# Moved weight splits in three blocks, and the gathered tokens' expert values summed pick by pick on VectorE

## The chip, the cores and the metric

The kernel runs on one core of a Trainium2 chip. The metric is the device time of one execution in microseconds (us). The five engines are called by their names or by the short forms of the profile: TensorE (PE, its weight loads PEld), VectorE (DVE), ScalarE (ACT), GpSimd (POOL), and SyncE (SP), which here only issues DMAs.

## The reference

Two transformer blocks run one after the other on one sequence of 512 tokens with 1024 features, all in float32.

The first block: RMS norm; one projection to a gated convolution branch (31 taps) and to an attention branch with 8 heads of stick-breaking attention; output projection and residual; RMS norm, a gated feed-forward part of width 2816 with a 3-tap convolution, and residual.

The second block: RMS norm and one projection; differential attention and a native sparse attention with a compressed, a selected and a window branch; sigmoid gates, output projection, residual; cross attention to 256 memory tokens; and then the part that the change is about, a layer of experts:

```python
s = jnp.einsum('thcd,hcnd->thcn', q, sub_keys)       # 8 heads, 2 halves, 128 keys
top_s, top_i = lax.top_k(s, 16)
cand = top_s[:, :, 0, :, None] + top_s[:, :, 1, None, :]
best_s, best_j = lax.top_k(cand, 16)                 # 16 experts of 128*128 a head and token
g = softmax(best_s)
act = gelu(einsum('cd,chkd->chk', x, u_tab[expert])) # 128 picks a token
out = einsum('chk,chkd->cd', g * act, v_tab[expert])
```

So each token picks 8 x 16 = 128 of 16384 experts, and its result is the sum over these picks of a weight times a row of 1024 values. At the end stands an RMS norm.

## The kernel before

**Number format and splits.** Nearly all products are made of three float32r matmuls: each operand is split into a high part (a rounded copy, ScalarE) and a low part (operand minus high part, GpSimd for weights, VectorE for activations), and `al*bh + ah*bl + ah*bh` is summed in PSUM. Weights come in blocks of up to 128x2048 into two buffers `raw[g % 2]`. `split_hi(act, g)` (L240 on) waits for the load and for TensorE to be done with block g - 2, and writes `w_hi`; `split_lo` (L253) writes `w_lo`, in the order of the blocks. TensorE (`linear_pe`, `products`, L261 to L263) waits for the low part of each block. As every engine executes its program in order, the place where a `split_hi` stands in ScalarE's program decides when the next block is ready.

**Places of these splits that matter here.** `block1_act`: the input projection `in_fm` (8 blocks of two 128-row tiles); for its first four pairs of tiles (j) ScalarE waits until VectorE has drained a pair, makes a sigmoid and then splits block j + 2; VectorE meanwhile works through a 31-tap convolution (`conv_dve`, L482), five taps behind each drained tile. `in_v`, the projection of the values, has eight tiles; `spread_pair` (L658) is a small matmul of TensorE behind tiles 2 to 5 that needs the reciprocal `rstd16` (L821) of VectorE, and `normalised` scales queries and keys by it. `first_scores` stands behind tile 6. `up0` is the first half of the feed-forward: behind each pair of tiles ScalarE makes a silu, a high part and then a split. `splits_gained` splits the next block and writes the high parts and squares of the residual for the next norm. `block2_act` holds the sigmoid of 24 gates (L1106), two exponentials (L1109, L1111) and `hidden(1)`, a gelu (L1096) that TensorE waits for (L1278). In the cross attention loop VectorE scales the exponentials of one unit (L1658), ScalarE exponentiates and copies the transposed ones; one weight split stands behind the loop's second step.

**The experts.** 384 of the 512 tokens (NT) are computed densely, the first 128 (GT) by gathers.

Dense, first half (the u stage): for each of 128 chunks c of 128 experts SP loads `u_raw` (512 KB), ScalarE and GpSimd split it, TensorE multiplies it with the 384 tokens (24 matmuls of 384 columns), ScalarE takes the gelu, SP stores it to a scratch (192 KB). Chunks 0 to PRE - 1 (PRE = 36) run while VectorE works out the picks (`places`, `mark_places`, `keys`, for four groups of 128 tokens); the next 72 chunks run between matmuls that build the table of gate weights (L2178, two batches of 8 tokens for three chunks), which needs `rows_b` of ScalarE (L2033) and `rows_a` of VectorE; the table goes to a scratch in pieces of 1 MB (`store_g`). The last 20 chunks stand alone. At FETCH_AT, chunk 120, SP begins to load what the second half needs.

Gathered tokens, first half: GpSimd issues 128 indirect DMAs (`gather_u`, L1918), one for each pick, that bring one row of 1024 values per token into a ring of seven buffers; `gathers_by(c)` says how many are issued by chunk c, and each stands in GpSimd's program behind `split_u_lo(c)`. Gather 4 waits until the keys of all four groups are there. VectorE makes the dot product of each row with the token (L2383, the token in PSUM). A gather waits for the dot seven before it.

Second half (the value stage): for each chunk c SP loads `h_raw` (192 KB, the stored gelu) and `v_raw` (512 KB), and for eight chunks at once `g_in` (1.5 MB of gate weights). VectorE multiplies h_raw by its gates (`weighted`, L2424) and makes its low part (`weighted_low`, L2428), ScalarE the high parts (L1943, L1952), GpSimd `v_lo` (L1947). All four have four buffers. TensorE adds 3 x 3 x 2 matmuls of 512 columns per chunk into three pairs of PSUM banks (`outputs`, L2208). ScalarE splits chunk c as soon as TensorE is done with chunk c - 4.

Gathered tokens, second half: for each of 32 steps i GpSimd issues four indirect DMAs (L1930) of rows of the value table, indexed by `idx_v`, the transpose of the picks, so that in each buffer all 128 partitions hold the picks of one token. TensorE multiplies them with 32 columns of a block-diagonal weight matrix `w_diag` (`gathered`, 16 matmuls, L2219) behind every fourth chunk, in plain float32, into the banks `y_acc`. `w_diag` comes from a memset of 128x4096 and four copies out of a transpose of the weights. At the very end VectorE adds the residual, and the last norm is made.

**What sets the order.** All of it is written out by hand, engine by engine, with counting semaphores; there is no planner. `peer_credits` gives the ring buffers their first credits.

The change touches, besides these places, `gather_v`, `ug_loaded` and the semaphores of the rows, `block3_pool`, `turn` (which transposed `idx_f` too), and `residual`, which takes the gathered tokens' sum out of PSUM.

## Time and profile before

| | us |
|---|---|
| three runs: median (lowest, highest) | 2587.88 (2580.64, 2592.19) |
| the profiled execution, its own time | 2588.76 |
| its span, first to last instruction | 2587.0 |
| TensorE busy | 2494.9 |
| VectorE busy | 1623.5 |
| GpSimd busy | 1363.2 |
| ScalarE busy | 1004.6 |
| data moved by DMA | 477.61 MB, mean 185 GB/s |

Busy time is the time in which an engine executes something; it contains stalls inside an instruction. The timeline and the chain of waits are in microseconds from the start of the span. "Idle before" names the engine and line whose completion ended an engine's idle time. The chain of waits is followed back from the last instruction, at each step to what released it. "PEclk" is the granted clock of TensorE as a share of its full 2.4 GHz; its other level is 1.2 GHz. The DMA share is the mean busy share of 16 DMA engines.

### The profile page before, as it was taken

Reading aid. Unit: us, or ns where it says so; the run is one execution under the profiler, and the core shown is the slowest. Engines: PE = TensorE matmul, PEld = TensorE weight load, DVE = VectorE, ACT = ScalarE, POOL = GpSimd, SP = SyncE. Lnnn points to the kernel's source line nnn. Section 1 sums busy time; section 2 is a strip of 40 time slices with the busy share of each in tenths; the row PEclk is TensorE's granted clock in tenths of the full one; section 3 lists DMA queues with packets and bytes.
Section 4 is the critical chain, followed back from the end, with each engine's and each line's share of the span. In section 5 each row is a group of like instructions: output and inputs, shape, how many; then the busy total and the mean of one; then the engine's idle time right before and its main releaser. Section 6 shows DMA issues by size and latency. Waiting matters only on the chain.

```text
span 2587.0 us, 34189 instructions
## 1 busy us (share of the span) xinstructions
PE 2494.9 (96%) x13105; PEld 2080.4 (80%) x13105; DVE 1623.5 (63%) x2822; ACT 1004.6 (39%) x1768; POOL 1363.2 (53%) x698
## 2 busy tenths in 40 slices
PE   6999899999999999998999989999999999999998
PEld 5765788888887666886899889999998677777776
DVE  4967654153224766645999967777746666666665
ACT  3236322123213655334444345555533233333333
POOL 3422355454432112442436666666677777777774
PEclk9989999999999999999999999999999999999999
DMA  3200222222421011322225579999999988888884
GB/s 133 81 33 17 74 91 91 102 97 83 180 98 50 17 36 47 123 105 82 82 89 174 186 243 319 332 331 331 332 357 341 345 329 310 313 303 326 313 311 179
DMA packets 151781, 477.61 MB, mean 185 GB/s; under 512 B 14688, under 2 KB 47840, under 8 KB 140640
## 3 DMA queue, kind: packets, MB, share of 16 engines
q1 hardware_dynamic: 114784, 341.64, 37.3%
q0 software_dynamic: 36864, 134.23, 14.4%
q8 instruction: 78, 1.28, 0.2%
q14 instruction: 55, 0.45, 0.1%
HBM read 423.39 MB, written 52.43 MB: 184 GB/s over the span
## 4 chain that ended last, share of the span: by engine, by line
PE 75%; DVE 16%; ACT 3%; DMA 2%; POOL 2%; issue 2%; SPq 0%; ACTq 0%; DVEq 0%
PE bank_pair L2208 19%; PE bank_pair L261 13%; PE bank_pair L263 13%; PE bank_pair L262 13%; PE bank_pair L2178 3%; DVE cacc L482 2%; PE bank_pair L2219 2%; PE bank_pair L1298 1%; PE bank_pair L684 1%; PE bank_pair L1333 1%; DMA u_raw<-expert_u 1%; POOL w_lo L253 1%; DVE one_hot L2325 1%; PE bank_pair L1349 1%; PE bank_pair L272 1%
## 5 line engine op out<-in xcount | busy, mean ns | idle before, releaser
L253 POOL TENSOR_TENSOR w_lo<-w_raw,w_hi 128x2048 fp32r<-128x2048 f32 (+2 forms) x95 | 420.4, 4426 | 597.6 <-ACT w_hi L248 597.4
L1905 POOL TENSOR_TENSOR u_lo<-u_raw,u_hi 128x1024 fp32r<-128x1024 f32 x128 | 313.3, 2448 | 192.5 <-ACT u_hi L1901 192.2
L1947 POOL TENSOR_TENSOR v_lo<-v_raw,v_hi 128x1024 fp32r<-128x1024 f32 x128 | 309.7, 2424 | 112.3 <-ACT v_hi L1943 111.7
L2428 DVE TENSOR_TENSOR h_lo<-h_raw,h_hi 128x384 fp32r<-128x384 f32 x128 | 251.5, 1965 | 184.7 <-ACT h_hi L1952 184.5
L261 PE MATMUL bank_pair<-uh,u_lo 128*128 128x384 f32 x1024 | 352.1, 344 | 13.9 <-POOL u_lo L1905 13.5
L263 PE MATMUL bank_pair<-uh,u_hi 128*128 128x384 f32 x1024 | 343.5, 335 | 0.0
L262 PE MATMUL bank_pair<-ul,u_hi 128*128 128x384 f32 x1024 | 343.5, 335 | 0.0
L1943 ACT ACTIVATE v_hi<-v_raw 128x1024 fp32r<-128x1024 f32 x128 | 135.6, 1060 | 384.5 <-PE bank_pair L2208 353.1
L248 ACT ACTIVATE w_hi<-w_raw 128x2048 fp32r<-128x2048 f32 (+2 forms) x96 | 174.6, 1819 | 274.3 <-PE bank_pair L263 258.9
L261 PE MATMUL bank_pair<-xh,w_lo 128*128 128x512 f32 x624 | 247.6, 397 | 18.8 <-POOL w_lo L253 16.7
L1901 ACT ACTIVATE u_hi<-u_raw 128x1024 fp32r<-128x1024 f32 x128 | 135.6, 1060 | 334.7 <-PE bank_pair L263 302.5
L263 PE MATMUL bank_pair<-xh,w_hi 128*128 128x512 f32 x624 | 245.0, 393 | 0.0
L262 PE MATMUL bank_pair<-xl,w_hi 128*128 128x512 f32 x624 | 244.8, 392 | 0.0
L2208 PE MATMUL bank_pair<-v_lo,h_hi 128*128 128x512 f32 x768 | 240.8, 395 | 1.3 <-DVE h_lo L2428 1.3
L2208 PE MATMUL bank_pair<-v_hi,h_lo 128*128 128x512 f32 x768 | 237.3, 390 | 0.0
L2208 PE MATMUL bank_pair<-v_hi,h_hi 128*128 128x512 f32 x768 | 236.9, 390 | 0.0
L261 PEld LDWEIGHTS bank_pair<-uh,u_lo 128*128 128x128 f32 x1024 | 193.6, 189 | 18.7 <-POOL u_lo L1905 16.4
L262 PEld LDWEIGHTS bank_pair<-ul,u_hi 128*128 128x128 f32 x1024 | 193.6, 189 | 0.0
L263 PEld LDWEIGHTS bank_pair<-uh,u_hi 128*128 128x128 f32 x1024 | 193.0, 188 | 0.0
L2208 PEld LDWEIGHTS bank_pair<-v_lo,h_hi 128*128 128x128 f32 x768 | 141.7, 188 | 55.4 <-issue 25.1
L2383 DVE CUSTOM_DVE_ANT_0 ug<-bank_pair,ug 128x1024 f32<-128x1024 f32 x128 | 151.7, 1218 | 46.2 <-DMA ug<-expert_u_rows,idx_u 46.2
L2208 PEld LDWEIGHTS bank_pair<-v_hi,h_lo 128*128 128x128 f32 x768 | 144.2, 188 | 30.9
(445 smaller groups left out, 5170.3 us busy)
## 6 DMA issues: line engine op xcount, KB each, us to landing
w_raw<-w_small SPq DMA_DIRECT2D x80, 1024.0 KB, 4.8
u_raw<-expert_u SPq DMA_DIRECT2D x128, 512.0 KB
v_raw<-expert_v SPq DMA_DIRECT2D x128, 512.0 KB, 6.5
h_scratch<-h_act SPq DMA_DIRECT2D x128, 192.0 KB
g_scratch<-stage SPq DMA_DIRECT2D x24, 1024.0 KB, 6.2
g_in<-g_scratch SPq DMA_DIRECT2D x16, 1536.0 KB, 13.4
h_raw<-h_scratch SPq DMA_DIRECT2D x128, 192.0 KB, 5.8
w_raw<-w_small SPq DMA_DIRECT2D x8, 768.0 KB, 4.2
```

The source lines that it names most:

```text
L248: act.activation(wh[g % 2][:, :n], raw[g % 2][:, :n], ACT.Copy).then_inc(sem("hi_done"), 1)
L253: pool.tensor_tensor(wl[g % 2][:, :n], raw[g % 2][:, :n], wh[g % 2][:, :n].bitcast(F32), ALU.subtract).then_inc(sem("lo_done"), 1)
L261: pe.matmul(out, al, bh, start=(k == 0), stop=False)
L262: pe.matmul(out, ah, bl, start=False, stop=False)
L263: last = pe.matmul(out, ah, bh, start=False, stop=(k == len(pairs) - 1))
L1901: act.activation(u_hi[c % 2][:, :, :], u_raw[c % 4][:, :, :], ACT.Copy).then_inc(sem("u_hi"), 1)
L1905: pool.tensor_tensor(u_lo[c % 2][:, :, :], u_raw[c % 4][:, :, :], u_hi[c % 2][:, :, :].bitcast(F32), ALU.subtract)\
L1943: act.activation(v_hi[c % 4][:, :], v_raw[c % 4][:, :], ACT.Copy).then_inc(sem("v_hi"), 1)
L1947: pool.tensor_tensor(v_lo[c % 4][:, :], v_raw[c % 4][:, :], v_hi[c % 4][:, :].bitcast(F32), ALU.subtract)\
L2208: last = pe.matmul(acc[tt][:, cols], h[s][:, tokens], v[s][:, cols], start=start and n == 0, stop=stop and n == 2)
L2383: dve.tensor_tensor_reduce(out=rows[:, :], in0=x_tok[:, :], in1=rows[:, :], scale=1.0, scalar=0.0, op0=ALU.mult, op1=ALU.add, accum_out=do ...
L2428: dve.tensor_tensor(h_lo[c % 4][:, :], h_raw[c % 4][:, :], h_hi[c % 4][:, :].bitcast(F32), ALU.subtract)\
```

## The change

In words, in the order of the program:

1. `splits_gained`: where a block has four tiles (`cross_o`), the split of the block after next stands before the fourth tile of the block, not before its first.
2. `in_fm`: block 2 is split ahead of `norm_std`; each later split stands one step earlier.
3. `in_v`: the spreads stand behind tiles 3 to 6, the first scores behind tile 6 want only six of eight scaled tiles; the last spread pair stands behind them and writes to two banks of `lin_bank`.
4. `up0`: block 2 is split right behind `norm_std`, each later one a step earlier.
5. Block 2: the two exponentials stand before the gate sigmoids, and VectorE waits for the gates where it uses them.
6. Cross attention: the second split of `cross_v` stands behind the loop.
7. Experts: PRE is 40 (20 single chunks at the end become 16), FETCH_AT stays at chunk 120, gathers of the first half go on from chunk 37, with 7 per 5 chunks instead of 4 per 3.
8. The rows of the value table are gathered with the index of the first half, one pick of all 128 tokens per DMA, into a ring of eight buffers: eight in the first four chunks, then as `rows_asked_by` says. VectorE multiplies each by the pick's weight (one scalar per partition) and adds it in PSUM, `picks_by(c)` of them by chunk c, from chunk 8 to 127. `gathered`, `w_diag`, `idx_v` and the transposes for them are gone.

```diff
@@ splits_gained
-                if b < t["nb"] - 1:
+                if b < t["nb"] - 1 and t["tiles"] < 4:
                     split_hi(act, t["block"] + b + 2)
                 for k in range(b * t["tiles"], (b + 1) * t["tiles"]):
+                    if b < t["nb"] - 1 and k % t["tiles"] == 3:
+                        split_hi(act, t["block"] + b + 2)
@@
-        SPREAD_TILES = (2, 3, 4, 5)
+        SPREAD_TILES = (3, 4, 5, 6)
 
         def spread_bank(n):
-            return att_bank[3 - n % 2]
+            return att_bank[3 - n % 2] if n < 6 else lin_bank[n - 6]
@@ block1_act
+            base = LAYER["in_fm"]["block"]
+            split_hi(act, base + 2)
             act.wait_ge(sem("consts"), N_CONST)
             norm_std(act, "n1", norm_stat1, S)
-            base = LAYER["in_fm"]["block"]
             for j in range(CT):
...
-                split_hi(act, base + j + 2)
+                split_hi(act, base + j + 3)
             for j in range(4):
                 if j < 3:
-                    split_hi(act, base + 4 + j + 2)
+                    split_hi(act, base + 4 + j + 3)
...
-            split_hi(act, base + 4 + 3 + 2)
@@
             norm_std(act, "n2", norm_stat2, S)
+            split_hi(act, LAYER["up0"]["block"] + 2)
...
-                    split_hi(act, up["block"] + b + 2)
+                    if half:
+                        split_hi(act, up["block"] + b + 2)
+                    elif b < FHALF[0] - 1:
+                        split_hi(act, up["block"] + b + 3)
@@ block1_pe
             def first_scores(pe):
-                pe.wait_ge(sem("qk_ready"), len(PAIR_ORDER))
+                pe.wait_ge(sem("qk_ready"), 6)
                 scores(0)
+                pe.wait_ge(sem("bank_free"), 4 + LAYER["in_v"]["tile"] + 6)
+                spread_pair(3)(pe)
...
-            pe.wait_ge(sem("bank_free"), 4 + LAYER["in_v"]["tile"] + 7)
+            wait(pe, ("bank_free", 4 + LAYER["in_v"]["tile"] + 7), ("qk_ready", len(PAIR_ORDER)))
             scores(1)
@@ block2_act
+            act.wait_ge(sem("lam_sum"), 1)
+            act.activation(lam_exp[:, :], att_bank[3][:, 0:2], ACT.Exp).then_inc(sem("lam_exp"), 1)
+            act.wait_ge(sem("cmp_sub"), 1)
+            act.activation(cmp_s[:, :, :, :], cmp_s[:, :, :, :], ACT.Exp).then_inc(sem("cmp_exp"), 1)
             norm_wait(act, "n3", "diag", 1, 1)
...
-            act.wait_ge(sem("lam_sum"), 1)
-            act.activation(lam_exp[:, :], att_bank[3][:, 0:2], ACT.Exp).then_inc(sem("lam_exp"), 1)
-            act.wait_ge(sem("cmp_sub"), 1)
-            act.activation(cmp_s[:, :, :, :], cmp_s[:, :, :, :], ACT.Exp).then_inc(sem("cmp_exp"), 1)
             hidden(1)
@@
-                if s == 1:
-                    splits("cross_v", 1)
...
+            splits("cross_v", 1)
             splits_gained(act, "cross_o", "n5", pq_h, "norm_ffn")
@@
             chain.link(dve.reciprocal(rec2, stat2))
+            dve.wait_ge(sem("bank_free"), 4 + MIXED)
             chain.link(dve.tensor_tensor(cmp_rec[:, :, :], cmp_rec[:, :, :], gates24[:, :, 0::3], ALU.mult))
@@
-        PRE = 36
+        PRE = 40
-        FETCH_AT = PRE + MID + 12
+        FETCH_AT = PRE + MID + 8
         def gathers_by(c):
 
-            if c < 33:
+            if c < 37:
                 return max(0, min(UG_EARLY, c - 18))
-            return min(P, UG_EARLY + (c - 31) * 4 // 3)
+            return min(P, UG_EARLY + (c - 35) * 7 // 5)
@@
+        def picks_by(c):
+
+            return max(0, min(P, (c - 7) * 16 // 15))
+
+        def rows_asked_by(c):
+
+            return min(len(vg), 2 * (c + 1)) if c < 10 else min(P, picks_by(c - 2) + len(vg))
+
+        def gather_v(pool, j):
+
+            b = j % len(vg)
+            if j == 0:
+                pool.wait_ge(sem("u_used"), 2 + NK)
+            if j >= len(vg):
+                pool.wait_ge(sem("vg_used"), j - len(vg) + 1)
+            pool.indirect_dma_start(vg[b][:, :], None, v_rows, bass.IndirectOffsetOnAxis(idx_u[:, j:j + 1], 0))\
+                .then_inc(sem(vg_loaded(j)[0]), 16)
@@ block3_pool
-            for k in range(QUADS):
-                for n in range(4):
-                    split_v_lo(pool, 4 * k + n)
-                for i in {0: (0,), 1: (1,), 2: (2, 3)}.get(k, (k + 1,)):
-                    if i < QUADS:
-                        gather_v(pool, i)
+            for c in range(NK):
+                split_v_lo(pool, c)
+                for j in range(rows_asked_by(c - 1), rows_asked_by(c)):
+                    gather_v(pool, j)
@@ block3_pe
-                if i == 0:
-                    pe.transpose(lin_bank[0][:, 3 * P:4 * P], idx_f[:, :], ident[:, :])
...
-            def gathered(i):
-
-                pe.wait_ge(sem("w_step"), 3)
-                pe.wait_ge(sem(f"vg_loaded{i % 2}"), 16 * VQ * (i // 2 + 1))
-                for half in range(2):
-                    for q in range(VQ):
-                        w = w_diag[:, (i * VQ + q) * 32:(i * VQ + q + 1) * 32]
-                        last = pe.matmul(y_acc[half][32 * q:32 * q + 32, :], w, vg[i % 2 * VQ + q][:, half * S:(half + 1) * S],
-                                         start=(i == 0), stop=(i == NK // VQ - 1))
-                last.then_inc(sem("vg_used"), 1)
@@ block3_dve
+            def picked(j):
+                b = j % len(vg)
+                wait(dve, vg_loaded(j))
+                w = w_tok[:, j:j + 1]
+                if j == 0:
+                    dve.wait_ge(sem("w_step"), 1)
+                    ins = dve.tensor_scalar(y_tok[:, :], vg[b][:, :], w, None, ALU.mult)
+                else:
+                    dve.wait_ge(sem("vg_used"), j)
+                    ins = dve.scalar_tensor_tensor(out=y_tok[:, :], in0=vg[b][:, :], scalar=w, in1=y_tok[:, :],
+                                                   op0=ALU.mult, op1=ALU.add)
+                ins.then_inc(sem("vg_used"), 1)
+
             weighted(0)
             for c in range(NK):
                 weighted(c + 1)
                 weighted_low(c)
-                if c == 3:
-                    dve.wait_ge(sem("u_lo"), 4 + NK)
-                    link(dve.memset(w_diag[:, :], 0.0))
...
+                for j in range(picks_by(c - 1), picks_by(c)):
+                    picked(j)
```

## Rows read from the trace of the kernel before

**Rows 1.** The page's first part: busy us (share of the span) xinstructions.

```profile
PE 2494.9 (96%) x13105; PEld 2080.4 (80%) x13105; DVE 1623.5 (63%) x2822; ACT 1004.6 (39%) x1768; POOL 1363.2 (53%) x698
```

**Rows 2.** Chain that ended last, value stage: start us, us, engine, output, line.

```profile
2042.61 1.85 PE bank_pair L2219 x16
2044.47 16.59 PE bank_pair L2208 x72
2579.74 1.24 DVE out_sb L2452
```

**Rows 3.** Instructions of L2208: ns min/median/max, first and last start us.

```profile
L2208 PE MATMUL bank_pair<-v_lo,h_hi x768: 388/389/505, 1984.3 to 2578.4; 128*128 128x512 f32 x192
```

**Rows 4.** Timeline of PE: start us, us, what, [idle before it <-who ended it].

```profile
47.72 0.79 PE L261 MATMUL bank_pair<-xh,w_lo 128*128 128x512 f32 x1 [9.23 <-POOL w_lo L253]
...
136.20 3.78 PE L658 MATMUL bank_pair<-rstd,head_spread 16*128 16x512 f32 x4 [3.77 <-DVE rstd L821]
...
320.65 0.79 PE L261 MATMUL bank_pair<-xh,w_lo 128*128 128x512 f32 x1 [6.92 <-POOL w_lo L253]
...
818.66 1.03 PE L1278 MATMUL bank_pair<-cmp_w,cmp_hid 128*16 128x64 f32 x8 [3.09 <-ACT cmp_hid L1096]
...
1181.15 0.69 PE L1422 MATMUL bank_pair<-ident,ca_e 128*128 128x128 f32 x2 [2.85 <-DVE ca_e L1658]
...
1220.74 0.79 PE L261 MATMUL bank_pair<-ca_h,w_lo 128*128 128x512 f32 x1 [2.43 <-DVE resid L759]
...
1489.23 0.69 PE L261 MATMUL bank_pair<-uh,u_lo 128*128 128x384 f32 x1 [4.22 <-POOL u_lo L1905]
...
1503.95 2.07 PE L2178 MATMUL bank_pair<-rows_b,rows_a 128*128 128x128 f32 x8 [4.10 <-ACT rows_b L2033]
...
2022.44 3.62 PE L2219 MATMUL bank_pair<-vg,w_diag 128*32 128x512 f32 x16 [2.41 <-DMA vg<-expert_v,idx_v]
```

**Rows 5.** Chain that ended last, around the first of these idle times.

```profile
39.25 0.69 DVE cpad L786
48.51 0.43 PE bank_pair L262
```

**Rows 6.** The same chain, before the second of them.

```profile
132.89 3.27 DVE rstd L821
```

**Rows 7.** Timeline of DVE, cross attention.

```profile
1177.06 4.04 DVE L1658 TENSOR_SCALAR ca_e<-ca_e,ca_stat 128x256 f32<-128x256 f32 x1
```

**Rows 8.** Three kinds of VectorE instruction: duration ns min/median/max.

```profile
L2383 DVE CUSTOM_DVE_ANT_0 ug<-bank_pair,ug x128: 1210/1219/1227, 1490.5 to 1972.6; 128x1024 f32<-128x1024 f32 x128
...
L482 DVE SCALAR_TENSOR_TENSOR cacc<-cpad,params_sb,cacc x120: 729/741/5098, 63.6 to 225.6; 128x512 f32<-128x512 f32 x120
...
L2428 DVE TENSOR_TENSOR h_lo<-h_raw,h_hi x128: 544/2450/7104, 1976.5 to 2560.5; 128x384 fp32r<-128x384 f32 x128
```

**Rows 9.** Groups, 2100 to 2500 us: count, busy us, mean ns, idle before.

```profile
L2428 DVE TENSOR_TENSOR h_lo<-h_raw,h_hi 128x384 fp32r<-128x384 f32 x87 | 172.4, 1982 | 134.0 <-ACT h_hi L1952 134.0
L2424 DVE TENSOR_TENSOR h_raw<-h_raw,g_in 128x384 f32<-128x384 f32 x87 | 94.9, 1091 | 6.6 <-DMA h_raw<-h_scratch 6.6
...
L1947 POOL TENSOR_TENSOR v_lo<-v_raw,v_hi 128x1024 fp32r<-128x1024 f32 x87 | 209.8, 2414 | 81.2 <-ACT v_hi L1943 80.8
L1930 POOL DMA_INDIRECT vg<-expert_v,idx_v x88 | 86.6, 984 | 24.0 <-issue 23.2
```

**Rows 10.** DMA of 2100 to 2560 us: total; issues, KB each, landing us.

```profile
DMA packets 51899, 142.06 MB, mean 309 GB/s; under 512 B 4912, under 2 KB 17328, under 8 KB 51873
v_raw<-expert_v SPq DMA_DIRECT2D x97, 512.0 KB, 7.3
g_in<-g_scratch SPq DMA_DIRECT2D x12, 1536.0 KB, 13.4
h_raw<-h_scratch SPq DMA_DIRECT2D x97, 192.0 KB, 4.9
```

**Rows 11.** A stretch: PE, PEld, DVE, ACT, POOL busy, PEclk, DMA share, GB/s.

```profile
1900.00:1950.00 50.00, 47.76 (x270) 46.26 (x269) 19.00 (x32) 16.26 (x22) 40.33 (x26) 1.00 1.03 402
```

More of the change, by code:

```diff
@@ L1754, in ug_loaded @@
             b, full = j % UG, 16 * (j // UG + 1)
-            return f"ug_loaded{b}", full
-        VQ = 4
+            return f"row_loaded{b}", full
         vg = [at(f"vg{i}", [P, D], o) for i, o in enumerate(
@@ L1919, in gather_u, with vg_loaded @@
                 .then_inc(sem(ug_loaded(j)[0]), 16)
[L1921 to L1931 removed]
+        def vg_loaded(j):
+            b = j % len(vg)
+            before = len(range(b, P, UG)) if b < UG else 0
+            return f"row_loaded{b}", 16 * (before + j // len(vg) + 1)
+        def picks_by(c):
+            return max(0, min(P, (c - 7) * 16 // 15))
+        def rows_asked_by(c):
+            return min(len(vg), 2 * (c + 1)) if c < 10 else min(P, picks_by(c - 2) + len(vg))
+        assert picks_by(NK - 1) == P and rows_asked_by(NK - 1) == P
+        def gather_v(pool, j):
+            b = j % len(vg)
+            if j == 0:
+                pool.wait_ge(sem("u_used"), 2 + NK)
+            if j >= len(vg):
+                pool.wait_ge(sem("vg_used"), j - len(vg) + 1)
+            pool.indirect_dma_start(vg[b][:, :], None, v_rows, bass.IndirectOffsetOnAxis(idx_u[:, j:j + 1], 0))\
+                .then_inc(sem(vg_loaded(j)[0]), 16)
         def gelu(act, c):
@@ L2230, in block3_pe @@
                     last.then_inc(sem("out_done"), 1)
-                    if c == 4:
-                        pe.wait_ge(sem("w_step"), 1)
-                        pe.transpose(y_acc[0][:, 0:P], w_tok[:, :], ident[:, :]).then_inc(sem("w_step"), 1)
-                if q == 1:
-                    gathered(0)
-                if q >= 1:
-                    gathered(q)
-            gathered(QUADS - 1)
             for c in range(NK - 4, NK):
```

27 lines of the change are left out of this document (5 added, 22 removed).

## The prediction

> **What bounds the kernel now.** I read the page first: TensorE is busy 96% of the span [rows 1], so a change pays where it takes TensorE work or TensorE idle time away. Second the chain of waits over the last stage, in which every chunk of experts' values is multiplied in. There it is TensorE alone, in a rhythm of 16.59 us for the 72 `outputs` matmuls of four chunks and 1.85 us for the 16 matmuls of one `gathered` step [rows 2]; nobody waits in between. Third the timeline of PE with its idle times, which shows where the splits come late [rows 4]. The reader should see in it that nearly all idle time lies in single gaps with one named releaser each.
>
> **The value stage.** Its first matmul starts at 1984.3 [rows 3] and VectorE takes the last result at 2579.7 [rows 2]: 595.4 us. Of this 32 x 16.59 = 530.9 are `outputs`, 32 x 1.85 = 59.2 are `gathered`, and the second `gathered` step also waited 2.4 us for its rows and then ran 3.62 instead of 1.85 us [rows 4], 4.2 us together; the 1.1 us left are two short waits. The change deletes `gathered`, with the wait, the transpose and the 4096-wide diagonal matrix. 59.2 + 4.2 = 63.4 us leave TensorE.
> What is added: 128 picks on VectorE, each 128x1024, one input in SBUF, the other and the output in PSUM. No row shows this form. Nearest is the dot of L2383, 128x1024 with one input in PSUM: 1219 ns, and never above 1227 though GpSimd was subtracting beside it [rows 8]. The other end is the multiply-add of L482 with both inputs in SBUF, 741 ns for half the elements and up to 5098 ns when it meets GpSimd [rows 8]. I take the dot, 1.25 us with the wait for the pick before. 16/15 pick per chunk is 1.33 us; TensorE will need 16.59/4 = 4.15 us per chunk.
> VectorE: it is now busy 1.98 + 1.09 = 3.07 us per chunk with h_lo and h_raw [rows 9]. With the picks that would be 4.40, over 4.15. But most of the 3.07 is stall: alone each takes about 0.55 us (the minimum of L2428 is 544 ns [rows 8]; the two have one form but for the output's type), and they are long where they meet GpSimd's v_lo (2.41 us [rows 9]). GpSimd's 2.41 and 1.1 of VectorE exclude each other, 3.5 of 4.15 us; the pick can run beside v_lo, and VectorE's work without stall is 1.1 + 1.33 = 2.4. A steady order exists: v_lo beside a pick, then h_raw and h_lo, then the next pick. h_lo also has three chunks (12 us) before TensorE needs it. So I price VectorE at nothing; if the stalls stay as they are, the stage is paced at 4.40, 128 x 0.25 = 32 us more.
> GpSimd: v_lo 2.41 and 16/15 gathers of 0.98 + 0.27 of issue [rows 9], 3.75 of 4.15 us. It fits, with little left. A gather waits for the pick eight before it, and v_lo is queued behind it; the program asks only for rows whose buffer was picked two chunks earlier, so this wait should be over.
> DMA: per chunk v_raw 524 KB, h_raw 197 KB, an eighth of g_in 197 KB [rows 10] and 16/15 row gather of 524 KB, 559 KB: 1.477 MB in 4.15 us is 356 GB/s. Now it is 309 GB/s [rows 10]. A stretch of 50 us ran at 402 GB/s [rows 11], so I price it at nothing; v_raw lands in 7.3 us and has about 13 us before it is late.
> The Trainium skill (DMA: Bandwidth & Descriptors, Specifications) puts the HBM limit of one core at about 358 GB/s. By it the stage would sit at its limit, with no reserve. The 402 GB/s of [rows 11], where most of the traffic is also reads, disagree with it, with one core at work.
> New cost at the start: two gathers now stand behind each of v_lo 0 to 3, where before all four v_lo came first. Two gathers are 2.5 us, v_lo with them 4.9 against 4.15: about 0.7 us late three times, 2 us. Bounds 0 and 5. Term: 63.4 - 2 = 61 us saved.
>
> **The moved splits.** Each removes a gap of TensorE and what the gap costs after it. After the first one the chain has the matmuls at 0.43 us [rows 5], the step of the lower of the engine's two clocks; at the full clock they take 16.59/72 = 0.23 [rows 2]. Some twelve ran so: 12 x 0.2 = 2.4 us.
> - in_fm: `split_hi(base + 2)` no longer stands behind the first sigmoid. The gap of 9.23 [rows 4] was ACT's split and then GpSimd's. The next limit is VectorE's drain of tile 0, done at 39.25 + 0.69 [rows 5]; the gap begins at 47.72 - 9.23 = 38.5, so 1.5 us stay. 7.7 + 2.4 = 10. VectorE's convolution, which paces the rest of in_fm, begins only after tile 5, so it moves along. Bounds 5 and 12.
> - in_v: the spreads stand one tile later, tile 3 fills the gap of 3.77 [rows 4]. VectorE's reciprocal ends at 132.89 + 3.27 = 136.2 [rows 6] and is not moved by this, and one more weight split may meet the convolution ahead of it. Gap and slow clock together are 7; I take 4, bounds 0 and 7. What is late next: the last pair's spread, with tile 7 still to cover it.
> - up0: `split_hi(block + 2)` right behind norm_std, no longer behind the whole chain of convolution, silu and product of the first pair of tiles; ScalarE and GpSimd then have the time of two tiles for it, which is more than they need. 6.92 [rows 4] + 2.4 = 9.3. ScalarE's next pieces wait for VectorE anyway. Bounds 6 and 10.
> - exps of the compressed branch before the gate sigmoids: the subtraction they need is done while TensorE still works on mix_tm, so they move beside it. hidden(1) no longer queues behind two exps and a table load; the gap of 3.09 [rows 4] shrinks by an estimated 2, and VectorE's chain of softmax steps behind it, which starts earlier, by a little more. Term 2.7, bounds 0 and 4.
> - cross attention: GpSimd's w_lo no longer meets the row scaling, which took 4.04 us for 256 columns [rows 7] (512 columns with two inputs take 741 ns [rows 8]) and made the gap of 2.85 [rows 4]; with the slow clock behind it 4.3. The split now comes behind the loop, with the first four tiles of cross_o to cover it. cross_o's split stands behind three gained tiles, not before the first: the gap of 2.43 [rows 4] and some slow matmuls go, 3.7. Together 8, bounds 3 and 10.
>
> **PRE 36 to 40, gathers from chunk 37.** At chunk 34 TensorE waited 4.22 us because GpSimd's u_lo stood behind gather 4, which waits for the last keys [rows 4]; that gather now stands four chunks later. 4.2 + 2.2 of slow clock, a little less than above as its tiles are shorter, = 6.4. The 4.10 us before the first table [rows 4] stay: ACT makes the rows only behind the gelu of the last chunk before it, wherever PRE is. The rate 7/5 instead of 4/3 adds 2% of traffic in the middle stage; store_g comes four chunks nearer to the fetch at 120, and SP waits for it there with the next u_raw queued behind it. Bounds of the whole: gain 8, loss 3.
>
> **Sum.** 61 + 10 + 4 + 9.3 + 2.7 + 8 + 6.4 = 101 us. The profiled execution took 2588.8 us (its span 2587.0 and 1.8 around it), 0.9 above the median of the runs shown, 2587.9. 2588.8 - 101 = 2487.8; against the median 2487. With every small piece a chance to fall short and none to give more, I say 2489.
>
> **Rivals.**
> A. The value stage gets a new pace. VectorE keeps its stalls (4.40 us per chunk) or the DMA settles at 340 GB/s (1.477 MB in 4.34 us): 25 to 32 us are given back, 2514 to 2521. For it: VectorE's sum above 4.15, GpSimd at 3.75, the DMA need 15% above today's. Against: buffers of four chunks and eight rows, the stretch at 402 GB/s. A half of it gives 2503.
> B. The early gaps close but a chain behind them takes the time back: VectorE's convolution in in_fm, the top-k chain that paces chunks 25 to 33, DMA at the end of the u stage. Then of the 40 us outside the value stage perhaps 15 remain: 2514.
> C. Slower: the pick behaves as L482, not as the dot, taking GpSimd's port for its SBUF operands. Then it waits out v_lo each time: 16/15 x (1.25 + 2.41) = 3.9, with 3.07 already there 7.0 us per chunk, 128 x 7.0 = 896 instead of 531, 2853. If all only exclude each other, 2.41 + 1.1 + 1.33 = 4.84 per chunk, 88 us more, 2577. It decides for slower from (531 + 101)/128 = 4.94 us per chunk on. Against it: the pick has one operand in SBUF, like the dot.
> The Trainium skill (SBUF: State Buffer, Who interferes with whom) says that a VectorE instruction with two SBUF inputs contends with a GpSimd instruction that reads SBUF, and one with at most one does not. The 1227 ns of the dot agree; no row has a pick with its output in PSUM.
> D. The change doesn't do what it says: rows arrive late because of the eight buffers, VectorE stands in a pick and h_lo behind it. A row is asked for 5.5 chunks (23 us) before its pick; with landings of some 10 us it holds. It would look like A.
>
> **How the numbers follow.** Forecast 0.64, with its own range 2478 to 2502 (the bounds of the small terms, not all at one end). A with D 0.18, B 0.12, C 0.03 (of it 0.02 slower), something unseen 0.03. The range 2474 to 2524 takes in A and B. What a measurement can tell from no change is 0.5%, 13 us: faster 0.96, same 0.02, slower 0.02.
>
> **What would show it.** In the profile after: no L2219, the chain in the value stage as L2208 without a break, 16.6 us per four chunks, the stage 533 us long; picks of 1.2 us; VectorE near full but mostly in stalls; DMA near 350 GB/s; TensorE idle below 3 us at the places of [rows 4], but 4 us before the first table. The prediction is wrong if L2208 shows waits for h_lo or v_lo in the value stage, or picks well above 1.3 us, or if gaps of the early stages return under other names.

## The result

The kernel before took 2585.18 us (median of 4 runs), the changed kernel 2504.29 us (2503.76 to 2509.48, 4 runs), ratio 0.968 [0.9644, 0.9715]. The forecast was 2489 with a range of 2474 to 2524. So the change makes the kernel faster, by 81 us in the medians and by 84.3 us between the two profiled executions (2588.8 and 2504.5), where the sum said 101. The table below accounts for the missing 17.

### The profile page after: what moved, and what is told of

The parts are those of the page before. It is cut to its first block, busy times and chain, and to the rows that moved or that the text cites. A ratio compares the mean times of both kernels' runs of the same rounds, so it can differ in the third digit from the quotient of the medians.

```text
span 2502.7 us, 33378 instructions
## 1 busy us (share of the span) xinstructions
PE 2422.7 (97%) x12591; PEld 2066.0 (83%) x12591; DVE 1729.9 (69%) x2944; ACT 1006.3 (40%) x1768; POOL 1376.9 (55%) x698
## 4 chain that ended last, share of the span: by engine, by line
PE 57%; DVE 22%; issue 9%; DMA 8%; POOL 2%; ACT 2%; SPq 0%; DVEq 0%; ACTq 0%
PE bank_pair L261 14%; PE bank_pair L262 13%; PE bank_pair L263 13%; DVE bank_pair L2435 4%; PE bank_pair L2193 3%; DMA h_raw<-h_scratch 3%; DVE h_lo L2423 2%; DVE cacc L484 2%; DMA u_raw<-expert_u 2%; DMA g_in<-g_scratch 1%; PE bank_pair L1305 1%; DVE one_hot L2321 1%; PE bank_pair L1340 1%; PE bank_pair L690 1%; PE bank_pair L272 1%
## 5 line engine op out<-in xcount | busy, mean ns | idle before, releaser
L2419 DVE TENSOR_TENSOR h_raw<-h_raw,g_in 128x384 f32<-128x384 f32 x128 | 263.3, 2057 | 39.8 <-DMA h_raw<-h_scratch 39.7
L2223 PEld LDWEIGHTS bank_pair<-v_hi,h_hi 128*128 128x128 f32 x768 | 144.7, 188 | 30.2
```

The costliest lines, as they stand in the source:

```text
L2223: last = pe.matmul(acc[tt][:, cols], h[s][:, tokens], v[s][:, cols], start=start and n == 0, stop=stop and n == 2)
L2419: dve.tensor_tensor(h, h, g_in[c // OCT % 2][:, :, c % OCT, :], ALU.mult).then_inc(sem("h_f"), 1)
```

## The profile after

First the page's line of busy times, which answers to [rows 1]:

```profile
PE 2422.7 (97%) x12591; PEld 2066.0 (83%) x12591; DVE 1729.9 (69%) x2944; ACT 1006.3 (40%) x1768; POOL 1376.9 (55%) x698
```

Then the value stage, by stretch (columns: window, its length, busy us and instructions of PE, PEld, DVE, ACT, POOL, the granted clock, the DMA engines' busy share, GB/s):

```profile
2000.00:2450.00 450.00, 450.00 (x1987) 372.59 (x1986) 433.66 (x340) 163.25 (x220) 392.68 (x228) 1.00 0.98 362
```

TensorE doesn't pause once in 450 us, beside a VectorE that is busy for 96% and DMA engines for 98%. The two costliest lines of VectorE in it, asked by line over the whole trace (duration in ns: shortest/median/longest, then the start of the first and the last, in us):

```profile
L2435 DVE SCALAR_TENSOR_TENSOR bank_pair<-vg,w_tok,bank_pair x127: 1274/1277/1290, 2001.0 to 2478.3; 128x1024 f32<-128x1024 f32 x127
L2419 DVE TENSOR_TENSOR h_raw<-h_raw,g_in x128: 543/2238/3343, 1950.0 to 2470.8; 128x384 f32<-128x384 f32 x128
```

The pick is 1.28 us, never more than 1.29 (forecast 1.25; the slower rival C is out). h_raw bears the stall: its median is four times its shortest, and in the timeline it stands beside GpSimd's v_lo (h_raw from 2242.05 for 3.33 us, v_lo from 2242.55 for 2.41).

The timeline of PE's waits, which answers to [rows 4] (start, duration, instruction; in brackets the idle time before it and who ended it):

```profile
40.00 0.50 PE L261 MATMUL bank_pair<-xh,w_lo 128*128 128x512 f32 x1 [1.51 <-DVE cpad L794]
117.45 3.60 PE L654 MATMUL bank_pair<-qk_sq,head_sum 128*16 128x512 f32 x4 [3.75 <-ACT qk_sq L527]
306.14 0.79 PE L261 MATMUL bank_pair<-xh,w_lo 128*128 128x512 f32 x1 [6.92 <-POOL w_lo L253]
802.23 0.62 PE L1285 MATMUL bank_pair<-cmp_w,cmp_hid 128*16 128x64 f32 x8 [1.09 <-ACT cmp_hid L1104]
806.23 0.49 PE L1305 MATMUL bank_pair<-ka,qa 64*128 64x128 f32 x4 [2.36 <-DVE cmp_pt L1538]
809.25 1.22 PE L1305 MATMUL bank_pair<-ka,qa 64*128 64x256 f32 x3 [1.63 <-DVE att_stat L1551]
1464.50 0.87 PE L2170 MATMUL bank_pair<-ident,chosen 128*128 128x128 f32 x3 [5.21 <-DVE chosen L2338]
1496.52 2.07 PE L2193 MATMUL bank_pair<-rows_b,rows_a 128*128 128x128 f32 x8 [4.13 <-ACT rows_b L2050]
1947.89 0.44 PE L261 MATMUL bank_pair<-uh,u_lo 128*128 128x384 f32 x1 [2.05 <-POOL u_lo L1910]
1968.01 0.73 PE L2223 MATMUL bank_pair<-v_lo,h_hi 128*128 128x512 f32 x2 [0.81 <-POOL v_lo L1966]
2477.19 0.70 PE L2223 MATMUL bank_pair<-v_lo,h_hi 128*128 128x512 f32 x2 [4.13 <-DVE h_lo L2423]
```

Gone against [rows 4]: 9.23, 3.77, both waits of the cross attention, 4.22 at chunk 34 and the wait for gathered rows. Stayed: 6.92 at up0, and 4.1 before the first table (as forecast). New: 3.75, 5.21, 4.13, and four short waits for v_lo at the start of the value stage, the first of which is shown.

Where the 84.3 us come from. The savings are differences of one event's start in the two traces, given in brackets or behind "to", before first. The first table comes at 1503.95 and 1496.52; in the changed kernel four more chunks of the u stage, 16.6 us, stand ahead of it and four fewer behind, so these are added and taken off:

| stretch | forecast | saved |
|---|---|---|
| start to the matmul that waits for mix_h (249.31, 234.79): in_fm, in_v | 14 | 14.5 |
| up0 | 9.3 | 0 |
| exps of the compressed branch, to 837.57 and 822.65 | 2.7 | 0.4 |
| cross attention, to 1403.86 and 1379.81 | 8 | 9.1 |
| PRE and gathers, to the first table, less the four chunks | 6.4 | 0 |
| end of the u stage, to the first value matmul (1984.3, 1962.9) | 0 | -2.7 |
| value stage (595.4, 532.5) | 61 | 63 |

## The experiments

**One half of the change at a time.** e1_value_only is the kernel before with the gathered values summed on VectorE, its splits, PRE and u gathers untouched; e2_splits_only the reverse, the changed kernel with the value stage, PRE and the u gathers taken back. The cores of the two, e1 against the kernel before and e2 against the changed one:

```diff
-                if q >= 1:
-                    gathered(q)
-            gathered(QUADS - 1)
...
+                for j in range(picks_by(c - 1), picks_by(c)):
+                    picked(j)
```

```diff
-                for j in range(picks_by(c - 1), picks_by(c)):
-                    picked(j)
...
+            gathered(QUADS - 1)
...
-        PRE = 40
+        PRE = 36
```

> Only the pick-by-pick sum of the gathered tokens, on the old order of everything else and PRE 36. My theory (the gathered matmuls were pure TensorE time, VectorE, GpSimd and DMA cover the picks): 59 + 4 us leave, 2 come back at the start of the value stage and some 5 at its end, where VectorE is late: about 58 to 62 us less than before, 2523 to 2529. Rival (part of the gain needs the other edits, by more DMA reserve in the value stage with the earlier gathers): under 50 us, above 2535.

> Only the moved splits of the two blocks, the spreads, the exponentials and the cross attention, on the old last block (PRE 36, matmul sum). Theory from the trace of the changed kernel: 24 us less than before, 14.5 of them by the attention of the first block, 0 in up0, 0.4 at the exponentials, 9 in the cross attention; 2562 to 2566. My prediction on record had 34 for these; the rival that it stands for (the loss lies in the last block, not here) gives 2554.

Measured beside a median of 2590.81 before: e1 2528.54, ratio 0.976 [0.9739, 0.9776], 62 us; e2 2566.70, 0.991 [0.9892, 0.9927], 24 us. The halves add up to 86, and the changed kernel's 2504.29 is 86 us under the same median, so they don't work against each other. The missing 17 us lie outside the value stage: the moved splits bring 24 where the sum had 34, and the 6.4 for PRE and the gathers, which e2 has not, did not come (e3).

**PRE and the gathers put back.**

```diff
-        PRE = 40
+        PRE = 36
...
-        FETCH_AT = PRE + MID + 8
+        FETCH_AT = PRE + MID + 12
...
-            if c < 37:
+            if c < 33:
...
-            return min(P, UG_EARLY + (c - 35) * 7 // 5)
+            return min(P, UG_EARLY + (c - 31) * 4 // 3)
```

> The changed kernel with PRE 36, 4 gathers per 3 chunks from chunk 33, as before. Theory (moving the gathers frees GpSimd, whose subtractions then meet VectorE's key reduction, so what TensorE gains behind gather 4 it loses at the turn of the keys): no change, within 4 us of the changed kernel, and in the trace the wait for chosen back at about 1 us and the one behind gather 4 back at about 4 us. Rival (my prediction): the edit is worth 6.4 us, so this kernel is 6 slower.

2505.70, 0.968 [0.9659, 0.9697]: the same as the changed kernel. In its trace the old pair of waits is back:

```profile
1456.88 0.52 PE L2170 MATMUL bank_pair<-ident,chosen 128*128 128x128 f32 x3 [1.12 <-DVE chosen L2338]
1461.63 0.69 PE L261 MATMUL bank_pair<-uh,u_lo 128*128 128x384 f32 x1 [4.23 <-POOL u_lo L1910]
```

1.12 + 4.23 in this order, 5.21 in the changed one: one wait changed its name. The edit can be read at its place too: from the matmul that waits for mix_h to the first value matmul it takes 1727.6 us here and 1728.1 in the changed kernel.

**Why it changed its name.** e7_hold_pool keeps PRE at 40 and only lets GpSimd ask for a row early, so that it stands still at chunk 33 again.

```diff
-                return max(0, min(UG_EARLY, c - 18))
+                return max(0, min(UG_EARLY, c - 18)) + (c >= 33)
```

> The changed kernel, PRE stays at 40, but from chunk 33 on each gather of u rows is asked for one chunk earlier, so that GpSimd stands waiting for the keys at chunk 33 as before the change and makes no u_lo meanwhile. Theory (the two engines' shared access to SBUF makes the key selection slow): the three reductions of the last key selection take 2.4 instead of 6.5 us, TensorE's wait for chosen is near 1.1 instead of 5.21 us, and a wait of about 4.2 us for u_lo stands behind it: total 2502 to 2507, no gain. Rival (it is PRE at 40, which puts other matmuls ahead of the last scores, that makes chosen late): the reductions stay at 6.5 and the wait at 5.2, with the u_lo wait added, 2508 to 2512.

First the changed kernel: VectorE's three folding additions of the last key selection (L2321), and GpSimd beside them:

```profile
1456.96 6.51 DVE L2321 TENSOR_TENSOR one_hot<-one_hot 128x2048 bf16<-128x2048 bf16 x3
1456.31 2.86 POOL L1910 TENSOR_TENSOR u_lo<-u_raw,u_hi 128x1024 fp32r<-128x1024 f32 x1 [1.53 <-ACT u_hi L1906]
1460.53 2.67 POOL L1910 TENSOR_TENSOR u_lo<-u_raw,u_hi 128x1024 fp32r<-128x1024 f32 x1 [1.35 <-ACT u_hi L1906]
```

Then e7_hold_pool, VectorE, GpSimd and TensorE:

```profile
1461.93 2.41 DVE L2321 TENSOR_TENSOR one_hot<-one_hot 128x2048 bf16<-128x2048 bf16 x3
1465.51 0.95 POOL L1923 DMA_INDIRECT ug<-expert_u_rows,idx_u  x1 [5.76 <-DVE chosen L2338]
1465.38 0.52 PE L2170 MATMUL bank_pair<-ident,chosen 128*128 128x128 f32 x3 [1.13 <-DVE chosen L2338]
1468.89 0.50 PE L261 MATMUL bank_pair<-uh,u_lo 128*128 128x384 f32 x1 [2.98 <-POOL u_lo L1910]
```

The additions fall from 6.51 to 2.41 us with nothing changed but GpSimd's standing still, and the wait of 5.21 to 1.13. The rival (PRE's order makes the keys late) is out. From the wait at 1441.69 (the last for u_lo before these) to the first table it takes 58.5 us, in the changed kernel 59.8 (from 1436.74). The run's 2508.24 (0.970 [0.9677, 0.9723]) can't tell 1.3 us from nothing.

**The third transpose of keys later.**

```diff
-        TURN_AT = (25, 29, 33)
+        TURN_AT = (25, 29, 36)
```

> The changed kernel with the third transpose of the chosen keys behind chunk 36 instead of chunk 33, some 12 us later on TensorE. Theory: TensorE's wait of 5.21 us for the last key selection goes, and the slow matmuls behind it (about 2 us): 5 to 7 us less, 2497 to 2499. Rival: the first gathers and the table's rows hang on that transpose, and what is won comes back as a longer wait before the first table (4.13 us now) or at GpSimd's u_lo behind the gathers: 2502 to 2506.

The wait of 5.21 is gone, one of 2.81 for u_lo at 1487.49 is in its place, 4.10 before the first table stays. The same stretch takes 56.9 us, 2.9 less. The time, 2508.10 (0.970 [0.9676, 0.9722]), missed the expected 2497 to 2499: elsewhere this run was slower. Its profile has TensorE at mix_h 5.25 us later than the changed kernel's, ahead of every edited line, and 6.5 instead of 4.13 us of waiting at the very end.

**up0.** ScalarE's split of the second block now starts at 287.46, early enough, as forecast. GpSimd's doesn't. In the changed kernel:

```profile
287.46 1.91 ACT L248 ACTIVATE w_hi<-w_raw 128x2048 fp32r<-128x2048 f32 x1
299.55 1.57 POOL L636 TENSOR_TENSOR fl<-f_out,fh 128x512 fp32r<-128x512 f32 x1 [15.46 <-ACT fh L599]
301.07 4.94 POOL L253 TENSOR_TENSOR w_lo<-w_raw,w_hi 128x2048 fp32r<-128x2048 f32 x1
```

GpSimd stood idle for 15.46 us, the last 10.2 of them with the finished w_hi (289.37) at hand, because `split_lo` is written behind its wait for the first product. e4_pool_up0 moves that:

```diff
             j = 0
+            split_lo(pool, LAYER["up0"]["block"] + 2)
...
-                    split_lo(pool, up["block"] + b + 2)
+                    if half:
+                        split_lo(pool, up["block"] + b + 2)
+                    elif b < FHALF[0] - 1:
+                        split_lo(pool, up["block"] + b + 3)
```

> The changed kernel with GpSimd's low parts of the up0 weights moved a step earlier too, as ScalarE's high parts are. Theory (the 6.92 us wait of TensorE stayed because GpSimd's split_lo stood behind the wait for ff_hi): the gap goes to under 0.5 us and 9 us leave in all with the slow clock behind it. Rival (TensorE then waits there for the next thing, bank or norm): gap stays over 3 us, gain under 5.

```profile
290.96 4.59 POOL L253 TENSOR_TENSOR w_lo<-w_raw,w_hi 128x2048 fp32r<-128x2048 f32 x1 [5.36 <-ACT w_hi L248]
301.06 1.60 POOL L637 TENSOR_TENSOR fl<-f_out,fh 128x512 fp32r<-128x512 f32 x1 [5.51 <-ACT fh L599]
```

TensorE waits there no more. From mix_h to cmp_hid it needs 558.2 us (236.32 to 794.57), the changed kernel 567.4: 9.2 saved, where the prediction had 9.3. In the time 5 arrived (2499.05, 0.965 [0.963, 0.9668]); in its trace a first load that landed 1.2 us later and a wait of 6.67 instead of 4.13 at the very end took most of the rest.

**The exps put back** (the four lines of the two `Exp` behind the sigmoids again, and VectorE's added wait out).

> The changed kernel with the two exps of the compressed branch behind the gate sigmoids again, as before the change. Theory (moving them only exchanged one wait for another, 0.4 us net): TensorE waits 3.1 us for cmp_hid and 1.5 for cmp_pt instead of 1.1, 2.4 and 1.6; the stretch between the waits for mix_h and for the first att_pt transpose (from 234.8 to 974.4 in the changed kernel) is 0 to 1 us longer. Rival (the move is worth the 2.7 us forecast): 2 to 3.5 us longer there. The total can't tell it, it varies by more.

```profile
803.44 0.62 PE L1285 MATMUL bank_pair<-cmp_w,cmp_hid 128*16 128x64 f32 x8 [3.09 <-ACT cmp_hid L1104]
```

With 1.54 for cmp_pt, and none for att_stat. The stretch from mix_h to the first att_pt takes 741.3 us, in the changed kernel 739.6, in the kernel before 740.0. So the edit is worth 1.7 by this run and 0.4 by before and after; it stands between the two expectations, and one execution doesn't settle it. Both are under the 2.7 forecast.

**The wait at the end.** In the kernel before, the last two `gathered` steps stood right ahead of the last four chunks:

```profile
2558.86 3.64 PE L2219 MATMUL bank_pair<-vg,w_diag 128*32 128x512 f32 x32
2563.10 0.70 PE L2208 MATMUL bank_pair<-v_lo,h_hi 128*128 128x512 f32 x2 [0.59 <-DVE h_lo L2428]
```

TensorE asks for h_lo and v_lo of all four chunks before the first matmul, and v_hi of chunk 127 can't begin before chunk 123 is done. The 3.64 us covered most of that: with the 0.59 behind them they make 4.23. Without them 4.13 are bare, and behind them the 72 matmuls take 18.22 us instead of 16.32. In six other runs of this value stage (e1, e3, e4, e5, e7, e9) the wait was 6.5 to 6.7. e12_tail_order asks chunk by chunk:

```diff
-            for c in range(NK - 4, NK):
-                outputs_ready(c)
             for tt in range(NT // P):
                 for c in range(NK - 4, NK):
+                    if tt == 0:
+                        outputs_ready(c)
...
```

> The changed kernel, but in the last four chunks TensorE waits for each chunk's h_lo and v_lo just ahead of that chunk's first matmuls, not for all four before the first. Theory (the wait near the end is one of program order: v_hi of chunk 127 may only start when chunk 123 is done, so v_lo and h_lo of it come 3.5 to 4 us later at the earliest, and the two gathered steps that stood there before the change, 3.64 us, covered it): the 18 matmuls of chunks 124 to 126 for the first tokens, 18 x 0.23 = 4.15 us, take the place of that cover; the wait of 4.13 to 6.5 us shrinks to 0 to 2.4, and the slow matmuls behind it (about 1.5 us) go or shrink: 4 to 6 us less than the changed kernel on this chip, 0.9655 to 0.967 of the kernel before. Rival (VectorE is behind by its own work or by late loads, whatever the order): the wait comes back in full at the last chunk, under 1 us less.

```profile
2475.15 0.70 PE L2223 MATMUL bank_pair<-v_lo,h_hi 128*128 128x512 f32 x2 [1.50 <-DVE h_lo L2423]
2479.43 0.70 PE L2223 MATMUL bank_pair<-v_lo,h_hi 128*128 128x512 f32 x2 [2.67 <-DVE h_lo L2423]
```

From the second value chunk's first matmul to the end of the last it takes 528.1 us; the six with a wait of 6.5 took 529.4 to 532.0, the changed kernel's own profile 527.4. The run's time is that of the changed kernel, 2504.29 (0.968 [0.9667, 0.9701]), so the expected 4 to 6 us did not come. With the floor of the order gone 4.17 us of waiting are left, for h_lo of chunks 125 and 126: VectorE is late by itself, as the rival of this run has it. Two of ScalarE's lines of the same trace suggest from where:

```profile
2449.58 1.06 ACT L1962 ACTIVATE v_hi<-v_raw 128x1024 fp32r<-128x1024 f32 x1 [7.25 <-DMA v_raw<-expert_v]
2474.57 0.52 ACT L1971 ACTIVATE h_hi<-h_raw 128x384 fp32r<-128x384 f32 x1 [3.88 <-DVE h_raw L2419]
```

Some 45 us before the end ScalarE stood idle for 7.25 us until a v_raw landed; in e5 the chain that ended last goes through a v_raw of 14.40 us (2434.86) at the same place. My reading, not shown, is that the chunks behind it then come close together, GpSimd's v_lo beside VectorE's h_raw, and that VectorE has not regained its lead when the last four chunks are due.

**DMA or VectorE?** Two kernels relieve one of them. e10_half_rows gathers only 64 of the 128 rows from pick 8 on, e11_half_picks adds only 512 of the 1024 columns.

```diff
+            r = P if j < len(vg) else P // 2
-            pool.indirect_dma_start(vg[b][:, :], None, v_rows, bass.IndirectOffsetOnAxis(idx_u[:, j:j + 1], 0))\
+            pool.indirect_dma_start(vg[b][0:r, :], None, v_rows, bass.IndirectOffsetOnAxis(idx_u[0:r, j:j + 1], 0))\
```

> The changed kernel, but from pick 8 on only the rows of tokens 0 to 63 are gathered (half of each gather's bytes; tokens 64 to 127 get old rows, so the sum of these is left out). Per chunk 280 KB less: 1.197 MB in 4.15 us, 289 GB/s instead of 356. Theory (the DMA queues are what lets VectorE fall behind): in the changed kernel VectorE waited 39.7 us for h_raw and TensorE 4.13 us for h_lo at 2477, with slow clock behind it; with less to move, the waits for h_raw nearly vanish (under 5 us), the wait for h_lo at the last four chunks is gone, and the time is 5 to 8 us below the changed kernel, 2497 to 2500. Rival (VectorE's own work with its port waits is the pace): waits for h_raw vanish but h_raw's own duration grows in their place, the wait for h_lo stays at 4 to 6.5 us, time 2503 to 2506.

> The changed kernel, but from pick 1 on only 512 of the 1024 columns are multiplied in (the other half of the sum is left out); all rows are still gathered whole. A pick falls from 1.28 to about 0.7 us, 0.6 us per chunk less on VectorE. Theory (DMA): VectorE waits longer for h_raw in place of it, some 40 + 70 us, and the wait for h_lo near the end is halved at most, 2500 to 2505. Rival (VectorE's own work): the wait for h_lo is gone, 5 to 8 us less, 2497 to 2500, while the waits for h_raw grow less than the picks shrink.

e10: 2509.51 (0.970 [0.9674, 0.9725]), a wait of 9.03 at the end. Both theories missed, and the window says why this was no relief:

```profile
2000.00:2450.00 450.00, 450.00 (x1987) 372.63 (x1986) 406.48 (x337) 166.40 (x219) 385.17 (x228) 1.00 1.01 291
```

The rate fell from 362 to 291 GB/s, the engines' busy share rose from 0.98 to 1.01, and ScalarE's waits for v_raw (2000 to 2500) from 41.7 to 175.2 us. A gather of half the rows does not cost half (the last section has its price). e11: 2509.20 (0.970 [0.9666, 0.9723]); the pick takes 744 ns, h_raw's median falls to 546 ns, VectorE waits 20.7 instead of 15.4 us for the loads, the end's wait is 4.13, the stretch to the end 528.1 us. Both expectations missed here too. And the relief was smaller than planned: h_lo took over the stall, its mean rose from 0.65 to 1.76 us, and VectorE's busy time from 2000 to 2450 fell by 22 us (433.7 to 411.6), 0.2 us per chunk and not 0.6. In the middle of the stage VectorE's work isn't the bound, as TensorE is busy for all 450 us in both. Whether it is what makes 6.5 of 4.13 at the end is not shown: e11 has 4.13, but so has the changed kernel's own profile, with whole picks. What costs the lead may be the DMA, as ScalarE's late v_raw suggests; no run relieved that, and it stays open.

**The sum in SBUF**, rival C made real.

```diff
-        x_tok = y_tok = bank_pair[2]
+        x_tok = bank_pair[2]
+        y_tok = at("y_tok", [P, D], RAW)
...
                     dve.wait_ge(sem("w_step"), 1)
+                    dve.wait_ge(sem("u_lo"), 4 + NK)
```

> The changed kernel, but the sum of the gathered values is kept in SBUF and not in PSUM, so that each pick has two inputs in SBUF (its first pick waits for the end of the u splits, as its place was theirs). This is the case that the slower rival of the prediction described. Theory (VectorE shares its way into SBUF with GpSimd only when it needs two SBUF inputs, and the PSUM sum is what saves the change): picks wait out v_lo, up to 3.7 us each instead of 1.28, VectorE needs 4.8 to 5.5 us per chunk, TensorE waits for h_lo all along, and the stage is 80 to 170 us longer: 2585 to 2670. Rival (it makes no difference where the sum lies): picks of 1.2 to 1.4 us, 2504 to 2512.

```profile
2050.00:2450.00 400.00, 380.41 (x1593) 295.97 (x1592) 399.23 (x272) 131.67 (x177) 348.23 (x184) 0.99 0.90 328
L2437 DVE SCALAR_TENSOR_TENSOR y_tok<-vg,w_tok,y_tok x127: 1270/1273/3956, 2003.2 to 2532.6; 128x1024 f32<-128x1024 f32 x127
```

One run of 2559.28: 55 us over the changed kernel, still 27 under the kernel before. VectorE is full (399 of 400 us), and TensorE waits for h_lo (32.5 us in 21 waits). The median pick is as short as in PSUM, 1273 ns, but some take 3956 (mean 1588 in this window, 1278 in the changed kernel), and GpSimd's v_lo goes from a mean of 2405 to 2623 ns. The stretch to the end is 580.9 instead of 527.4 us. Both expectations missed: the place of the sum matters, by less than I had it.

**The three fixes together.**

> The changed kernel with three fixes: GpSimd splits the second block of up0 ahead of its wait for the first feed-forward product (as in e4_pool_up0), the third transpose of chosen keys behind chunk 36 (as in e5_turn_late), and the last four chunks' waits one by one (as in e12_tail_order). Theory, from the places alone: 9.2 us at up0, 2.9 us ahead of the first table, 4 to 6 at the end, together 16 to 18 under the changed kernel: 2487 to 2490, 0.962 of the kernel before. Rival: the gains of the parts are not additive, since the end of the u stage runs at the DMA's pace (410 GB/s) and takes back a part: 2492 to 2497.

2489.37 (2488.33 to 2493.79), 0.963 [0.9617, 0.9645], beside a median of 2586.14 before. 15 us under the changed kernel, at the upper edge of the theory, under the rival. The wait at up0 and the one for keys are gone, 2.16 us are left at the end, and from the second value chunk's first matmul to the end of the last it takes 525.3 us, less than in any other run of this value stage (the changed kernel 527.4, e12 528.1). It is the fastest kernel of this study.

## Why the prediction was right, and where it was off

- **The forecast as a whole.** Of the 101 us 84 came. 2504 lies just outside the 2478 to 2502 of the forecast's own path and inside 2474 to 2524 because that range left room for rivals A and B; what happened is B in part (a gap of up0 stayed, two gaps returned under other names). Two of the signs by which the prediction was to be wrong did appear: waits for v_lo and h_lo in the value stage (2.8 and 4.13 us) and gaps of the early stages under other names (3.75, 5.21).
- **What bounds the kernel.** Right. The time followed the waits of TensorE, and e1 and e2 add up.
- **Value stage, 61.** 63 measured, by two errors that cancel, so the closeness is luck. It also hangs on the two profiles: e2, with the value stage of before, took 593.0 instead of 595.4 us for it, and the six runs that wait 6.5 us at the end took 534.5 to 537.1 instead of 532.5. Between these the saving is 56 to 61 us. Taken apart, on the first two profiles: the `gathered` step was counted by its 1.85 us in the chain. ScalarE's v_hi, which follows each chunk's end, shows the true price. The kernel before, one cycle of four chunks:

```profile
2241.47 1.06 ACT L1943 ACTIVATE v_hi<-v_raw 128x1024 fp32r<-128x1024 f32 x1 [2.61 <-PE bank_pair L2208]
2245.55 1.06 ACT L1943 ACTIVATE v_hi<-v_raw 128x1024 fp32r<-128x1024 f32 x1 [2.61 <-PE bank_pair L2208]
2251.75 1.06 ACT L1943 ACTIVATE v_hi<-v_raw 128x1024 fp32r<-128x1024 f32 x1 [4.73 <-PE bank_pair L2208]
```

 Chunks are 4.08 us apart, and 6.20 where `gathered` lies between: 2.12 for it, 0.27 more than its matmuls' own time. In the changed kernel they are 4.08 all along, 16.32 for four and not 16.59:

```profile
2240.59 1.06 ACT L1962 ACTIVATE v_hi<-v_raw 128x1024 fp32r<-128x1024 f32 x1 [2.61 <-PE bank_pair L2223]
2244.67 1.06 ACT L1962 ACTIVATE v_hi<-v_raw 128x1024 fp32r<-128x1024 f32 x1 [2.61 <-PE bank_pair L2223]
```

 32 x 0.27 = 8.6 us more won than the sum had. Given back were 4.13 + 1.9 at the end, and at the start 2.8 us of four waits for v_lo (0.81, 0.63, 0.48, 0.83) with 1.3 of slower matmuls between them, where the sum had 2: 63.4 + 8.6 - 6.0 - 4.1 = 62. The step that failed: "63.4 us leave TensorE", with nothing asked about what the removed matmuls had covered. For in_fm and in_v the prediction does ask what is late next; here it doesn't.
- **VectorE, GpSimd, DMA priced at nothing.** Held for 450 us, at 362 GB/s against a need of 356 (1.477 MB in 4.15 us; in 4.08 us it is 362). VectorE's stalls moved from h_lo to h_raw and none fell on the pick, as argued. Rival A did not happen as a pace; a remnant of it is the lost lead at the end.
- **The limit of about 358 GB/s** (the Trainium skill, DMA: Bandwidth & Descriptors, Specifications). As a limit for one core at work the trace disagrees with it: 362 GB/s over 450 us, and 410 from 1900 to 1950. With two cores at work nothing was run.
- **in_fm, 10.** Right: 1.51 us stay at cpad, against 1.5, and the first head sum starts at 108.4 instead of 119.4. **in_v, 4**: its wait of 3.77 went, but 3.75 appeared at the last head sums (117.45). TensorE came 11.0 us sooner; the last drain of queries and keys, which VectorE makes between the taps of its convolution and whose squares the head sums need, came only 7.1 sooner (123.2, 116.1). This is rival B in small. At the wait of 1.58 us behind it (174.70, 163.49) 11.2 of the forecast 14 are saved. That the stretch still shows 14.5 is a matter of the clock: 3.3 of it lie between 165 and 240, and three later profiles with the changed order (e5, e11, best3) did not have them.
- **up0, 9.3.** Wrong, 0, for one step: "ScalarE and GpSimd then have the time of two tiles for it" took GpSimd's program order for granted. Only ScalarE's program was followed and changed. Mechanism and size were right once GpSimd's split was moved as well (9.2).
- **exps, 2.7.** Forecast too high: 0.4 to 1.7. The chain behind it started earlier and met GpSimd's w_lo: VectorE's slope product (one input, 0.41 us at its shortest) took 2.85 instead of 1.87 us, and TensorE's waits became 1.09, 2.36 and 1.63 instead of 3.09 and 1.54.
- **cross attention, 8.** 9.1, right.
- **PRE and gathers, 6.4.** Wrong, 0. The gather was indeed what held GpSimd, as put. But its standing still was what let VectorE select the last keys in 2.41 us. Freed, GpSimd makes u_lo beside it, and the selection takes 6.51 (e7).
- **End of the u stage.** Not in the sum; 2.7 between the two profiles. TensorE's waits for u_lo behind the first table come to 7.3 us before and 6.9 after, but the last 50 us before the first value matmul ran at a granted clock of 0.93 (1912 to 1962) and not 1.00 (1934 to 1984), an estimated 3.5 us. The edit is not shown to be the cause: from the first table to the first value matmul the kernel before took 480.3 us, but e1 took 483.7 and e2 482.7 with the same u stage as it, and the changed kernel 483.0 with the four chunks added. So the kernel before had a good execution there.
- **Rival C** was excluded for the right reason. The Trainium skill (SBUF — State Buffer, Who interferes with whom) has a VectorE instruction with two SBUF inputs contend with a GpSimd instruction that reads SBUF, and not one with at most one input outside the 2-port modes; the pick into PSUM (1290 ns at most) and the pick into SBUF (up to 3956) agree. The prediction left the exception of these modes out; instructions with one input that did grow beside w_lo are the slope product above and the row scaling of [rows 7]. C's price, 4.84 us per chunk, was too high: e6, a single run, goes at 4.50 (its stretch is 53.5 us longer over some 128 chunks, 4.08 + 0.42), and stays faster than the kernel before.

## What to carry to other kernels

Before a block of matmuls is deleted, look at what was becoming ready while it ran: it may have been the only cover of a wait that no view shows yet. When a split or any two-engine step is moved, move it on both engines' programs, and check each one's order by itself. An engine that stands idle on a wait may be what keeps its neighbour's instructions short (2.41 against 6.51 us in e7); filling its idle time can cost the neighbour as much as it gains.

## What was unexpected of the hardware

- The same stretch of the same instructions, from the wait at L677 to mix_h, takes 71.3 us in some profiles (the changed kernel, e2, e3, e4, e9, e12 among them) and 74.6 in others (before, e1, e5, e11, best3), with a granted clock in 165 to 240 of 1.00 in the first and 0.95 in the second, 0.97 in best3; e7 lies between, with 72.9 us and 0.98. The engine had waited 1.58 us ahead of it in all of them. Between e3 and the changed kernel, the stretch before it (117.5 to 163.5) differs by 4 us too (42.1 and 46.0 us). With a first load that lands at 12.2 or at 13.3 us, this is why an edit of 2 to 5 us must be read at its place and not from the total. What decides which of the two comes stays open.
- Gathers of 64 rows instead of 128 moved 30.2 instead of 61.3 MB in 450 us but took 26.8% instead of 36.3% of the DMA engines' time, and the plain loads beside them rose from 61.5% to 74.3% for the same 100 MB.
